# First layer: two row blocks of the next query ahead of the first score, and two more between the last two scores

## The reference

```python
q, k, v = jnp.split(h @ w_qkv, 3, axis=-1)      # 16 half heads of 64
qx, kx = axial_rope(qx, rows, cols), axial_rope(kx, rows, cols)
s = jnp.einsum('bqnd,bknd->bnqk', q, k) * scale
p = jax.nn.softmax(s, axis=-1)                   # latent queries see all 512 tokens,
a = p[:, :, 0] - lam * p[:, :, 1]                # context queries the 256 of the context
o = rms_norm(jnp.einsum('bhqk,bkhe->bqhe', a, v), subln_g) * (1.0 - lam_init)
```

## Time and profile before

| | |
|---|---|
| median of the runs | 2443.85 us |
| profiled execution | 2444.69 us |
| its span, first to last instruction | 2442.7 us |
| mean granted TensorE clock | 0.999 |
| PE busy | 2401.5 us (98%) |
| DVE busy | 1313.9 us (54%) |
| ACT busy | 1001.3 us (41%) |
| POOL busy | 1106.9 us (45%) |

### The profile page before, as it was taken

The page is one execution under the profiler, slowest core; times in us unless marked ns, Lnnn a source line. Parts: engine busy times, 40 slices in busy tenths (PEclk is TensorE's granted clock), DMA queues, the critical chain, the costliest instruction groups (busy, mean ns, idle before and its releaser), DMA issues.

```text
span 2442.7 us, 37465 instructions
## 1 busy us (share of the span) xinstructions
PE 2401.5 (98%) x12338; PEld 1980.5 (81%) x12338; DVE 1313.9 (54%) x2343; ACT 1001.3 (41%) x2023; POOL 1106.9 (45%) x839
## 2 busy tenths in 40 slices
PE   9999999999999999999999999999999999999998
PEld 4666888888888888898888887778888888778998
DVE  8889875557254434356565143655766524475321
ACT  3566433332343343343323244664323324466553
POOL 0422445454444334435445443223544543436896
PEclk9999999999999999999999999999999999999999
DMA  8472445556322222326555323322555532323664
GB/s 326 122 146 90 143 171 182 198 173 225 106 87 78 78 72 83 94 88 214 199 206 183 109 79 97 82 81 96 206 206 198 183 109 83 99 78 118 182 182 130
DMA packets 121637, 340.62 MB, mean 139 GB/s; under 512 B 35537, under 2 KB 42961, under 8 KB 120913
## 3 DMA queue, kind: packets, MB, share of 16 engines
q1 hardware_dynamic: 113522, 333.97, 42.0%
q10 hardware_dynamic: 8032, 5.52, 1.5%
HBM read 334.76 MB, written 4.69 MB: 139 GB/s over the span
## 4 chain that ended last, share of the span: by engine, by line
PE 49%; issue 33%; POOL 12%; DVE 3%; ACT 2%; POOLq 0%; DMA 0%; DVEq 0%; ACTq 0%; SPq 0%
PE low_banks L635 39%; POOL w_lo L628 12%; PE high_banks L635 10%; DVE h_lo L1968 1%; DVE tmp L1949 1%; DVE ssum_rstd L1805 0%; ACT w_hi L1280 0%; ACT e_x L1443 0%; DVE rot L2143 0%; DMA ada_raw<-in_ada_w 0%; DVE ssum_rstd L1937 0%; POOLq L627 0%; DVE xT L1908 0%; ACT h_hi L1321 0%; ACT lnm L1304 0%
## 5 line engine op out<-in xcount | busy, mean ns | idle before, releaser
L628 POOL TENSOR_TENSOR w_lo<-w_raw,w_hi 128x512 fp32r<-128x512 f32 x832 | 1106.5, 1357 | 1316.9 <-ACT w_hi L1280 1316.2
L635 PE MATMUL low_banks<-h_hi,w_hi 128*128 128x512 f32 (+2 forms) x1792 | 639.7, 357 | 5.0 <-POOL w_lo L628 1.8
L1280 ACT ACTIVATE w_hi<-w_raw 128x512 fp32r<-128x512 f32 x832 | 473.9, 624 | 396.8 <-PE low_banks L635 191.8
L635 PE MATMUL low_banks<-h_lo,w_hi 128*128 128x512 f32 (+2 forms) x1792 | 632.3, 353 | 0.0
L635 PE MATMUL low_banks<-h_hi,w_lo 128*128 128x512 f32 (+2 forms) x1792 | 630.8, 353 | 0.0
L1805 DVE SCALAR_TENSOR_TENSOR ssum_rstd<-ada_raw,high_banks 128x1024 f32<-128x1024 f32 x304 | 370.7, 1220 | 44.3 <-DMA ada_raw<-in_ada_w 35.3
L635 PEld LDWEIGHTS low_banks<-h_hi,w_hi 128*128 128x128 f32 x1792 | 338.0, 189 | 60.7 <-issue 4.8
L635 PEld LDWEIGHTS low_banks<-h_lo,w_hi 128*128 128x128 f32 x1792 | 338.2, 189 | 46.5 <-issue 1.0
L635 PEld LDWEIGHTS low_banks<-h_hi,w_lo 128*128 128x128 f32 x1792 | 337.2, 189 | 46.5
L1713 ACT ACTIVATE lnm<-low_banks 128x512 f32<-128x512 f32 x66 | 39.4, 597 | 378.2 <-PE low_banks L635 378.2
L2465 DVE TENSOR_TENSOR tmp<-low_banks,lnm 128x512 f32<-128x512 f32 x66 | 45.6, 692 | 211.3 <-ACT lnm L1713 207.7
(11 more groups left out here) (279 smaller groups left out, 3792.7 us busy)
## 6 DMA issues: line engine op xcount, KB each, us to landing
w_raw<-in_weights SPq DMA_DIRECT2D x424, 512.0 KB, 3.8
ada_raw<-in_ada_w SPq DMA_DIRECT2D x152, 512.0 KB, 3.9
ada_first<-in_ada_w SPq DMA_DIRECT2D x22, 512.0 KB, 10.0
v_all<-in_ada_w SPq DMA_DIRECT2D x12, 512.0 KB, 4.3
bias<-rpb_skew SPq DMA_DIRECT2D x64, 64.0 KB, 2.4
rpb_skew<-rpb_rows ACTq DMA_DIRECT2D x1, 3556.0 KB, 36.8
ada_rest<-in_ada_w SPq DMA_DIRECT2D x6, 512.0 KB, 13.4
cond_l<-in_cond SPq DMA_DIRECT2D x3, 1024.0 KB
```

Of the source, the lines that this page charges most:

```text
L628: nc.gpsimd.tensor_tensor(out=w_lo[:, r, part], in0=w_raw[:, r, part], in1=w_hi[:, r, part], op=ALU.subtract).then_inc(lo_ready, 1)
L635: return nc.tensor.matmul(dst, lhsT, rhs, start=start, stop=stop, **kw)
L1280: nc.scalar.activation(w_hi[:, r, part], w_raw[:, r, part], ACT.Copy).then_inc(hi_ready, 1)
```

## The change

In tiles 1 to 6 of the first layer, two row blocks of the next tile's query (blocks 0 and 1, six matmuls) are put between the weighted sum and the wait for the scores, behind waits of their own, for the rotation of this tile's query and for its copy on ScalarE, since both read bank 6. The two row blocks ahead of score 3 are now blocks 2 and 3. From tile 2 on, the query that is left over from the tile before has four row blocks and not six.

```diff
                 def tile_da(t, slot, place):
                     if place >= 2:
-                        ahead = Q_BETWEEN if L.zq else Q_AHEAD
+                        ahead = 2 * Q_BETWEEN if L.zq else Q_AHEAD
                         unit(t * 2 + n, slot, bank[6], H, L.W, tiles=range(ahead, KT)).then_inc(unit_used, 1)
...
+                    elif place < 3:
+
+                        pe.wait_ge(L.qk_dve, t * 2 + 1)
+                        pe.wait_ge(L.qk_act, t * 2 + 1)
+                        unit(t * 2 + (n + 2), slot + 2, bank[6], H, L.W, tiles=range(Q_BETWEEN))
+
                     pe.wait_ge(L.qk_dve, t * 2 + 2)
                     pe.wait_ge(L.qk_act, (t + 1) * (1 + L.zq))
                     for j in score_order(L):
                         if j == o_bank and place >= 1:
                             if L.zq and place < 3:
-                                unit(t * 2 + (n + 2), slot + 2, bank[6], H, L.W, tiles=range(Q_BETWEEN))
+                                unit(t * 2 + (n + 2), slot + 2, bank[6], H, L.W,
+                                     tiles=range(Q_BETWEEN, 2 * Q_BETWEEN))
                             pe.wait_ge(L.y_ready, t)
                         score(j)
```

## The result

The changed kernel takes 2459.44 us (median of five runs, 2456.24 to 2462.67) against 2444.06 us (five runs of the kernel before, measured beside it): a ratio of 1.0061, 95% interval 1.0047 to 1.0076. It is 15.4 us slower; the forecast was 4.1 us more, in a range that ended at 2449.8. One execution of the kernel before, among those of the experiments, took 8358.47 us; it counts as a slow run and stands in no comparison. The profiled execution of the changed kernel took 2457.99 us, span 2456.2 us against 2442.7. Lines behind the edit have moved by seven: the products are L1885, the key's rotation ends in L2154.

What follows compares the result with a forecast made beforehand. The bound was taken as the loop from key through scores and score 3, then VectorE to the next key. Collisions of 0.94 + 1.06 + 1.04 + 0.94 plus 0.15 made +4.13 us: 2448.0 us, range 2443.5 to 2449.8.

Steps and rivals of the forecast that it cites:

- What bounds the attention: First layer's attention: TensorE from key to score 3, then VectorE to the next key, set the pace; moved work gains nothing.
- The collisions: Tiles 4 to 7: GpSimd's earlier differences stretch VectorE's last product ahead of the key, +0.94, 1.06, 1.04 and 0.94 us.
- The break of 0.31 us per group: Tiles 1 to 6: each group of six matmuls put ahead of the scores costs TensorE up to 0.31 us more.
- +0.15 in tile 3: Tile 3: TensorE is free 0.14 us after the old start of the scores, which goes through: +0.15 us, bounds 0 and 0.3.
- Above, a whole difference of 1.26 us in each of the four, and 0.3 + 0.5, 5.8 us.: Upper bound of the loss: a full GpSimd difference in tiles 4 to 7, plus upper bounds of tiles 3 and 1.
- waits of 2.0 to 3.8 us: TensorE's waits for the rotated key: 2.0 to 2.4 us in tiles 4 to 6, 3.8 in tile 7.
- PE hides none of it: Tiles 4 to 7: TensorE already waits for the key, so the delay of VectorE's products goes through in full.
- More: Rival: further collisions in tiles 2 and 3 or behind the key, one or two at about 1 us, 2449 to 2451 us; chance 0.11.

Runs made afterwards that it cites:

- experiment 3: Kernel before, with two more VectorE multiplications out of PSUM ahead of the key's rotation in tiles 4 to 7: 2452.79 us.
- the first filled gap: Changed kernel with eight more matmuls (result unused) ahead of the wait for the key in tiles 4 to 7: 2451.98 us.
- the last one of experiment 6: Changed kernel with two row blocks ahead of the scores, none ahead of score 3, GpSimd's differences held back, one product moved behind the key: 2437.76 us.
- experiment 2: Changed kernel with unused matmuls ahead of the wait for the key in tiles 4 to 7: eight each, 2451.98 us; 9, 14, 9 and 15, 2449.66 us.
- experiment 6: Gate (GpSimd's differences wait for mean square's matmul) on the changed kernel 2444.42 us; with a product moved behind the key 2438.37, on the kernel before 2438.50, two-blocks-only 2437.76.

## Why the prediction was wrong

- *What bounds the attention.* Right. The loop (key, scores, score 3, VectorE, key) holds to 0.02 us a tile (experiment 3), and no part of the moved work shortened it.
- *The collisions.* Right in all four places, priced at 0.94, 1.06, 1.04 and 0.94, measured 0.95, 1.06, 1.09, 0.95. The order at tiles 5 and 6, argued from 0.06 and 0.08 us, came out as computed. Left out was the small modulation sum behind the last product of tile 5, which reads two SBUF operands as well: 0.94 us.
- *The break of 0.31 us per group, and +0.15 in tile 3.* Too high. TensorE's own work between score 0 of tile 3 and that of tile 4 is 23.14 - 2.53 = 20.61 us against 22.21 - 1.65 = 20.56: about 0.05. Tile 3's scores came at no delay, and tile 2 waited 0.92 us and not 0.3.
- *"Above, a whole difference of 1.26 us in each of the four, and 0.3 + 0.5, 5.8 us."* This is the step that failed: the sum and its upper bound have no term for the clock. They ran over instructions that take longer or wait, and took TensorE's matmuls at the length of the rows of before. Those rows are all from a granted clock of 1.00, behind waits of at most 1.65 us. I forecast waits of 2.0 to 3.8 us and did not ask what the matmuls behind them would take; "PE hides none of it" should have gone on to the clock. The missing term is 8.0 us in the profiled run (3.20, 3.19 and 1.65), and 9.8 us by filling the gaps; with the gaps filled, and so without it, the kernel took 2449.66 us, just inside the range. The trace of before had a sign of it: TensorE's last matmul ends at 2435.3 us, and the granted clock falls to 0.50 between 2438 and 2440.
- *"More": 0.11, ending at 2451.* The rival was one of further collisions, so neither its place nor its price was the one that came.

## What to carry to other kernels

Work put into an idle gap gained nothing here, since the gap is the slack of another engine's loop; it only moved what hangs on that work, the start of GpSimd, which then met VectorE on its critical stretch. Ask of every wait that a forecast lengthens what TensorE's clock does behind it, and put that in the range. The remedy lay in the loop: one product off it, and GpSimd held to a stretch in which VectorE reads PSUM, gave 6 us for two small edits. The moved product without the gate was not run, nor was the gate alone on the kernel before.

## What the hardware showed that I had not expected

The thirteen profiled executions (the two kernels and the eleven experiments) have 61 waits of TensorE for the key in the first layer. Behind the 44 of up to 1.65 us the clock never fell. Behind the seven of 2.84, 2.85, 3.46, 3.60, 3.78, 3.79 and 3.80 us it fell every time. In between it went either way: it fell behind 1.92, 2.18, 2.20 and 2.53, and held behind 2.31, 2.33, 2.39, 2.46, 2.54 and 2.56. So the length of the wait alone does not decide there. Runs of one kernel with such waits spread over up to 8.6 us (the first filled gap), where those of the kernel before spread over at most 2.8 within one group and those of the last one of experiment 6 over 1.3. What TensorE does before these waits differs little: twelve transposes of 128 columns and eight matmuls of the weighted sum, in the changed orders followed by six of the query (not in tile 7), in experiment 2 by the unused ones as well. What tells a fall from no fall in the middle stays open. A fall cost 1.3 to 5.0 us from score 0 to score 3, by how much of the time behind the wait ran at 0.50: some 3.4 us in tile 7 of the changed kernel (1.65 more), some 6.8 in its tiles 4 and 5 (3.2 more), over 10 in tile 4 of the kernel with the change in tiles 1 to 3 (5.0 more). In two of the traces of experiment 6 the clock also fell once ahead of the attention (0.55 from 20 to 22 us in that of the changed order with gate and moved product).

A VectorE operation of eight columns, 0.17 us long, took 1.11 us when GpSimd was ahead of it (tile 5 of the changed kernel). The Trainium skill's rule on the shared port pair (SBUF — State Buffer, "Who interferes with whom") goes by the number of SBUF inputs and not by size, and this row bears it out; a count of collisions has to include the smallest operation.
